# The MLP's way down by seven products of sums of quarters

## The reference, cut to what matters

```python
x = x + squared_relu_mlp(rms_norm(x, mlp_norm[l]), w_up[l], w_down[l])     # l = 0, 1

def rms_norm(x, g):
    return x * lax.rsqrt(jnp.mean(x * x, axis=-1, keepdims=True) + EPS) * g

def squared_relu_mlp(h, w_up, w_down):                   # w_up 1024 x 4096, w_down 4096 x 1024
    return jnp.square(jax.nn.relu(h @ w_up)) @ w_down
```

## Time and profile before

| what | us |
| --- | --- |
| median of three runs | 3433.12 |
| lowest, highest run | 3431.18, 3434.05 |
| profiled execution, span from the first to the last instruction | 3430.4 |
| PE busy | 3379.4 (99%) |
| DVE, POOL, ACT busy | 1962.6, 1260.6, 1205.7 |

### The profile page before, as it was taken

One profiled execution on the slowest core, in us unless ns is written; L12 is line 12 of the kernel. 1 busy time (PEld: TensorE's weight loads), 2 busy tenths in 40 slices (PEclk: granted clock), 3 DMA queues, 4 the chain that ended last, 5 costly groups with the idle time before them and its releaser, 6 DMA issues.

```text
span 3430.4 us, 43111 instructions
## 1 busy us (share of the span) xinstructions
PE 3379.4 (99%) x16026; PEld 2788.4 (81%) x16026; DVE 1962.6 (57%) x2418; ACT 1205.7 (35%) x2072; POOL 1260.6 (37%) x828
## 2 busy tenths in 40 slices
PE   8999999999999999999999999999999999999999
PEld 7778888888888887777888888887888888778887
DVE  6666662844454477884384444457746546545445
ACT  6446651422222245764142222224524233102011
POOL 1121214444445440024344445453435345323340
PEclk9999999999999999999999999999999999999999
DMA  5010012111111121111211111113111111111241
GB/s 214 21 42 18 24 58 86 49 50 50 50 49 50 54 108 60 46 46 65 78 49 50 50 49 50 60 58 107 37 59 58 43 61 45 64 46 62 93 148 66
DMA packets 67634, 211.84 MB, mean 62 GB/s; under 512 B 7280, under 2 KB 11888, under 8 KB 65680
## 3 DMA queue, kind: packets, MB, share of 16 engines
q1 hardware_dynamic: 56848, 165.04, 14.6%
q10 hardware_dynamic: 10624, 44.63, 3.6%
HBM read 186.32 MB, written 22.02 MB: 61 GB/s over the span
## 4 chain that ended last, share of the span: by engine, by line
PE 92%; DVE 5%; issue 1%; POOL 1%; ACT 1%; DMA 1%; ACTq 0%; DVEq 0%; SPq 0%; POOLq 0%
PE G L885 37%; PE G L1303 20%; PE AUX L1253 17%; PE G L1545 3%; PE G L1124 2%; PE AUX L1186 2%; PE AUX L1424 2%; PE AUX L1322 2%; PE AUX L1176 1%; PE G L1007 1%; PE AUX L1166 1%; PE AUX L1053 1%; PE AUX L1303 1%; PE AUX L1506 1%; DVE probs L2553 1%
## 5 line engine op out<-in xcount | busy, mean ns | idle before, releaser
L885 PE MATMUL G<-Hhi,whi 128*128 128x512 f32 x1552 | 631.6, 407 | 7.3 <-DVE Hlo L2682 2.8
L885 PE MATMUL G<-Hhi,wlo 128*128 128x512 f32 x1552 | 605.9, 390 | 0.0
L885 PE MATMUL G<-Hlo,whi 128*128 128x512 f32 x1552 | 605.4, 390 | 0.0
L685 POOL CAST whi<-wraw 128x1024 fp32r<-128x1024 f32 (+1 forms) x123 | 135.6, 1102 | 1101.4 <-PE G L885 592.7
L1303 PE MATMUL G<-u_hi,slot_hi 128*128 128x512 f32 x992 | 387.7, 391 | 0.0
L1303 PE MATMUL G<-u_lo,slot_hi 128*128 128x512 f32 x992 | 386.2, 389 | 0.0
L1303 PE MATMUL G<-u_hi,slot_lo 128*128 128x512 f32 x992 | 386.1, 389 | 0.0
L885 PEld LDWEIGHTS G<-Hhi,whi 128*128 128x128 f32 x1552 | 292.1, 188 | 74.4 <-issue 7.1
L734 POOL TENSOR_TENSOR slot_lo<-raw_down,slot_hi 128x512 fp32r<-128x512 f32 x144 | 190.2, 1321 | 416.4 <-ACT slot_hi L1923 416.2
L885 PEld LDWEIGHTS G<-Hlo,whi 128*128 128x128 f32 x1552 | 292.3, 188 | 62.5 <-issue 5.7
L885 PEld LDWEIGHTS G<-Hhi,wlo 128*128 128x128 f32 x1552 | 291.7, 188 | 61.8
(11 more groups left out here) (463 smaller groups left out, 6890.8 us busy)
## 6 DMA issues: line engine op xcount, KB each, us to landing
wraw<-wjobs SPq DMA_DIRECT2D x148, 512.0 KB, 3.4
raw_down<-down_pairs SPq DMA_DIRECT2D x64, 512.0 KB, 3.4
raw_up<-up_units SPq DMA_DIRECT2D x30, 512.0 KB, 3.7
raw_up<-up_units SPq DMA_DIRECT2D x44, 256.0 KB, 3.3
mw_raw<-wjobs SPq DMA_DIRECT2D x16, 512.0 KB, 5.2
scratch<-X ACTq DMA_DIRECT2D x2, 4096.0 KB, 13.0
gate_tiles<-gate_st ACTq DMA_DIRECT2D x16, 512.0 KB, 4.1
T<-gate_tiles ACTq DMA_DIRECT2D x16, 512.0 KB, 3.5
```

The lines of the kernel that those rows point to most:

```text
L685: pool.tensor_copy(whi[:, par, 0:kt], wraw[:, par, 0:kt]).then_inc(w_hi, 1)
L885: mm = pe.matmul(G[:, par if psum is None else psum, cols], w[:, par, k, :], x[:, k, cols], start=(i == 0 and j == 0), stop=(i == kt - 1 a ...
```

## The change

In chunks 1 to 6 of both layers the way down is made as the way up: the 512 x 1024 piece of u (two units of 256 hidden features) and the matching piece of w_down are cut into quarters, and each of two groups g of output features (256 of each half) takes seven products (`unit_down`) instead of eight. A product is 2 x 2 x 3 = 12 matmuls into 1024 columns of G. `unit_up` replaces `unit` in chunks 1 to 7. In the middle chunks it ends in seven matrices per unit h, each 128 x 512: the blocks b11, b22, b21 of u and the sums t1 = b11 - b12, t2 = b22 + t1, t3 = b22 - b12, t4 = b21 - t2 (`total`, tiles d_sum), their high parts by ScalarE (`high_of_u`, tiles d_hi) and their low parts by VectorE (`low_of_u`, tiles d_lo in the place of d_sum). Each block is squared in place in SBUF (`square`). `add_product` adds each of the fourteen bank contents to a quarter of X; p1, p6, p7 and p4 accumulate in one bank pair, p5 and p3 in the other, and a product that goes on in a bank waits until VectorE has added what stood there.

The weights of the way down come as two more units, through the same raw buffers and `unit_weights` on GpSimd: per unit s1, s3, low of p1, s2, low, low of p6 (p6 comes third in each order), s4 and the remaining lows. `high` and `ahead` on ScalarE go over 28 uses a chunk.

The room for d_hi and d_lo is taken from t4 and from T: b21 and t4 of the input now share one 16 KB place. Both are written once to HBM (operand_tiles) during chunk 0, and `load_shared` fetches the one that is needed next: 2 MB, as four DMAs, in each unit of chunks 1 to 7, after its second product; it is used by that unit's last product (p2 or p4) and by the second product of the next unit.

The factor r2 is no longer applied to each chunk's sum: in chunk 0 X is multiplied by mean square + eps before the first sum is added, chunks 0 to 7 are added unscaled, and after chunk 7 X is multiplied by the reciprocal. The reciprocal stands after chunk 0's additions. Chunks 0 and 7 keep the plain way down; in chunk 7 `finish` makes the four low parts at each unit's end, and ScalarE's copies into T in the second unit wait for all four of the first.

The diff, cut to its core (`after(j, n)` waits for product j and n copies; `factor` is the former `product` with `load_shared`'s semaphore):

```diff
+FACTORS = {"p1": ("a11", "b11"), "p2": ("a12", "b21"), "p3": ("s4", "b22"), "p4": ("a22", "t4"),
+           "p5": ("s1", "t1"), "p6": ("s2", "t2"), "p7": ("s3", "t3")}
+UP_ORDER = (("p1", "p4", "p6", "p5", "p7", "p3", "p2"), ("p1", "p2", "p6", "p5", "p7", "p3", "p4"))
+DOWN_ORDER = ("p1", "p5", "p6", "p3", "p7", "p2", "p4")
+CHAINED = ("p1", "p6", "p7", "p4")
...
+LOW_ORDER = (("t3", "b11", "t1", "b22", "b21", "t2", "t4"), ("b11", "t1", "t2", "b22", "t3", "b21", "t4"))
...
+            def load_shared(n):
+                for half in range(2):
+                    ks = slice(2 * half, 2 * half + 2)
+                    for part in range(2):
+                        sp.dma_start(b21[part][:, ks, :].bitcast(F32), operand_tiles[n, part][:, ks, :]).then_inc(shared_in[half], 16)
...
+                for c in range(1, CHUNKS):
+                    for h in range(2):
+                        sp.wait_ge(m_used, use_of(l, c, h, 1) + 1)
+                        load_shared(1 - h)
+                        if c not in WHOLE:
+                            sp.wait_ge(m_lo, use_of(l, c, h, PRODUCTS - 1) + 1)
+                            load_unit(l, c, 2 + h)
...
+                    else:
+                        pe.wait_ge(m_exit, read)
+                        factor(c, h, 1, 2, True)
+                        pe.wait_ge(m_x, copied + 1)
+                        factor(c, h, 2, a, False)
+                        factor(c, h, 3, 1, True)
+                        pe.wait_ge(m_x, copied + 2)
+                        factor(c, h, 4, a, False)
+                        pe.wait_ge(m_x, copied + 3)
+                        factor(c, h, 5, 1, False)
+                        pe.wait_ge(m_exit, read + 2)
+                        factor(c, h, 6, a, False)
...
+                def unit_down(c, g):
+                    for j, name in enumerate(DOWN_ORDER):
+                        n, op = use_of(l, c, 2 + g, j), FACTORS[name][1]
+                        par, start = g if name in CHAINED else 1 - g, name in ("p1", "p5", "p2")
+                        if name in ("p6", "p7", "p4"):
+                            pe.wait_ge(m_out, added(l, c, g, {"p6": "p1", "p7": "p6", "p4": "p7"}[name]))
+                        elif name in ("p3", "p2"):
+                            pe.wait_ge(m_out, added(l, c, g, {"p3": "p5", "p2": "p3"}[name]))
...
+                        for h in range(2):
+                            if g == 0:
+                                pe.wait_ge(m_ul, f_low(l, c, h, op))
+                            for i in range(2):
+                                w = slice((2 * i + h) * P, (2 * i + h + 1) * P)
+                                for s, (a, x) in enumerate(((slot_hi, d_hi), (slot_hi, d_lo), (slot_lo, d_hi))):
+                                    mm = pe.matmul(G[:, par, i * HALF:(i + 1) * HALF], a[slot_of(n)][:, w], x[h][op][:],
+                                                   start=(start and h == 0 and s == 0), stop=(h == 1 and s == 2),
+                                                   skip_group_check=not start)
+                        mm.then_inc(m_used, 1)
...
+                    copies = ({"p1": ("b11", 0), "p4": ("b21", 2), "p6": ("b12", 0), "p5": ("b22", 1)} if h == 0 else
+                              {"p1": ("b11", 3), "p6": ("b12", 3), "p5": ("b22", 1)})
+                    for j, name in enumerate(UP_ORDER[h]):
+                        n = use_of(l, c, h, j)
+                        if name in copies:
+                            block, bank = copies[name]
+                            act.wait_ge(m_used, n + 1)
+                            if whole and h:
+                                act.wait_ge(m_ul, tiles_to(l, c, 1))
+                            act.copy(block_of_u(c, h, block), AUX[:, bank, :]).then_inc(m_x, 1)
+                        ahead(n)
+                        if h == 0:
+                            if j == 5:
+                                high_of_u(c, 0, "b22", "b21")
+                            elif j == 6:
+                                high_of_u(c, 0, *(("b12", "b11") if whole else ("t3",)))
+                        elif j == 0 and not whole:
+                            high_of_u(c, 0, "b11", "t1", "t2", "t4")
+                        elif j == 2:
+                            high_of_u(c, 1, "b11")
+                        elif j == 5:
+                            high_of_u(c, 1, "b22")
+                        elif j == 6:
+                            high_of_u(c, 1, *(("b12", "b21") if whole else ("t1", "t2", "t3")))
...
+                        for j in range(2 * PRODUCTS):
+                            ahead(use_of(l, c, 2, j))
+                            if j == 0:
+                                high_of_u(c, 1, "b21", "t4")
...
-                chain.link(dve.tensor_tensor(bank, bank, r2[:], ALU.mult))
-                dve.tensor_tensor(X[:, m, :], bank, X[:, m, :], ALU.add).then_inc(m_out, 1)
+                if c == 0:
+                    chain.link(dve.tensor_tensor(X[:, m, :], X[:, m, :], r2[:], ALU.mult))
+                    dve.wait_ge(m_used, use_of(l, c, 2, m) + 1)
+                    dve.tensor_tensor(X[:, m, :], bank, X[:, m, :], ALU.add).then_inc(m_out, 1)
+                else:
+                    dve.wait_ge(m_used, use_of(l, c, 2, m) + 1)
+                    chain.link(dve.tensor_tensor(X[:, m, :], bank, X[:, m, :], ALU.add))
+                    dve.tensor_tensor(X[:, m, :], X[:, m, :], r2[:], ALU.mult).then_inc(m_out, 1)
...
+                    if h == 0:
+                        after(4, 4)
+                        dve.tensor_tensor(b22_, a, b22_, ALU.subtract).then_inc(m_exit, 1)
+                        dve.tensor_tensor(b21_, a, b21_, ALU.add).then_inc(m_exit, 1)
+                        square("b22", 1)
+                        square("b21", 2)
+                        after(5, 4)
+                        dve.tensor_tensor(b12_, b12_, d, ALU.subtract).then_inc(m_exit, 1)
+                        square("b12", 3)
+                        total("t3", "b22", "b12", ALU.subtract, "b12")
+                        after(6, 4)
+                        dve.tensor_tensor(b11_, e, b11_, ALU.add).then_inc(m_exit, 1)
+                        square("b11", 4)
+                        total("t1", "b11", "b12", ALU.subtract, "b11")
+                        total("t2", "b22", "t1", ALU.add, "t1")
+                        total("t4", "b21", "t2", ALU.subtract, "t2")
+                        if whole:
+                            finish()
+                        else:
+                            dve.wait_ge(h_sums, f_sum(l, c, h, "t4"))
+                            low_of_u(*LOW_ORDER[0])
...
+                    after(1, 1)
+                    dve.tensor_tensor(b11_, e, b11_, ALU.add).then_inc(m_exit, 1)
+                    square("b11", 1)
+                    after(4, 3)
+                    dve.tensor_tensor(b22_, a, b22_, ALU.subtract).then_inc(m_exit, 1)
+                    square("b22", 2)
+                    after(5, 3)
+                    dve.tensor_tensor(b12_, b12_, d, ALU.subtract).then_inc(m_exit, 1)
+                    square("b12", 3)
+                    total("t1", "b11", "b12", ALU.subtract, "b12")
+                    total("t2", "b22", "t1", ALU.add, "t1")
+                    if not whole:
+                        low_of_u("b11")
+                    total("t3", "b22", "b12", ALU.subtract, "b12")
+                    if not whole:
+                        dve.wait_ge(h_sums, f_sum(l, c, h, "t3"))
+                        low_of_u("t1")
+                    after(6, 3)
+                    chain.link(dve.tensor_scalar(b21_, a, 0.0, None, ALU.max))
+                    dve.scalar_tensor_tensor(b21_, a, 0.0, b21_, ALU.max, ALU.mult).then_inc(h_sums, 1)
+                    total("t4", "b21", "t2", ALU.subtract, "b21")
+                    if whole:
+                        finish()
+                        return
+                    dve.wait_ge(h_sums, f_sum(l, c, h, "t4"))
+                    low_of_u("t2")
+                    add_product(c, 0, 0)
+                    low_of_u("b22")
+                    add_product(c, 0, 1)
+                    low_of_u("t3", "b21")
+                    add_product(c, 0, 2)
+                    low_of_u("t4")
...
+                    if name in ("p5", "p3"):
+                        ins = dve.tensor_tensor(x, x, bank, ALU.subtract)
+                    else:
+                        ins = dve.tensor_tensor(x, bank, x, ALU.add)
+                    ins.then_inc(m_out, 1)
```

More of the change, by code:

```diff
@@ L84 @@
 PRODUCTS = 7
-CHUNK_USES = 2 * PRODUCTS + KT
-MLP_USES = CHUNKS * CHUNK_USES
+WHOLE = (0, CHUNKS - 1)
+MIDDLE = CHUNKS - len(WHOLE)
+CHUNK_USES = [2 * PRODUCTS + (KT if c in WHOLE else 2 * PRODUCTS) for c in range(CHUNKS)]
+USES_BEFORE = [sum(CHUNK_USES[:c]) for c in range(CHUNKS)]
+MLP_USES = sum(CHUNK_USES)
 BLOCKS = ("11", "22", "12", "21")
@@ L397, in build, with block_of_u @@
```

(54 more changed lines are left out.)

362 lines of the change are left out of this document (269 added, 93 removed).

## The result

The changed kernel takes 3524.26 us (median of 4 runs, 3523.11 to 3525.39), the kernel before 3432.69 in the runs beside them (4 runs): a ratio of 1.0268, 95% interval 1.0253 to 1.0283. It is slower by 92 us; 3509 was predicted, with 3405 to 3545 as the range.

The account below looks back on a forecast made before the run. TensorE, busy 99%, was taken as the bound; fewer matmuls but new waits on VectorE and ScalarE: 3430.4 + 66 (middle chunks) + 7.8 (chunk 7) + 2 (last tile) = 3506, plus 2.7 to the runs' median: 3509 us, range 3405 to 3545.

Parts of the forecast that it names:

- The lock: VectorE operations with two SBUF inputs take turns with GpSimd's instructions: one of each costs 1.29 + 0.42 = 1.71 us.
- The walk: Step-by-step timing of one middle chunk from its first up unit: 10.98 us of TensorE waits, chunk 87.3 us, 5.5 more.
- Its 3.37 us: Unit 2's product 6 waits for ScalarE's copy of p5's bank, behind the cast of b11: 36.65 instead of 33.28.
- the 0.64 of b11's bank: Second unit's product 2 overwrites the bank of b11, so it starts at 22.40 instead of 21.76: 0.64 us wait.
- The 1.07 for p1's weight: On a middle chunk's way down, product p1 waits 1.07 us for its weight's low, ending at 43.06.
- The 0.68 for the low of t1: On a middle chunk's way down, p5's second half waits 0.68 us for the low of t1, at 50.42.
- Chunk 7: Copy into T waits for all four lows, 2.6 us; last lows end 1.3 late: 3.9 a layer, 7.8 in all.
- The tail: Product with r2 moves from PSUM to two SBUF operands, hidden until the last tile: 1 us a layer, 2 in all.
- items at nothing: Chunk 0's multiply of X, the 6.55 us reciprocal in chunk 1, and the operand stream and its writing: all expected hidden.
- The first: Rival: GpSimd's instructions slip past while VectorE waits for products, TensorE stays the bound: 77.2 us a chunk, 3380; chance 0.22.
- The second: Rival: ScalarE's cast of b11 is in time, waits of 4.5 to 8 us a chunk: 3431 to 3473; chance 0.12.
- The third: Rival: the streamed half lands late, last product of the first unit waits 2.3 us, fourteen times: 3541; chance 0.06.

Follow-up runs that it names:

- the last experiment: Changed kernel with t1 to t4 and squared b12 in PSUM, unit 1's lows later, unit 2 in TensorE's order, chunk 7's unit 2 blocks placed apart: 3375.33 us, 0.9833.
- the fifth run: Changed kernel with the differences t1 to t4 and the squared b12 kept in idle PSUM banks, all work still done: 3422.57 us, 0.9969 of the kernel before.
- the sixth run: Changed kernel with t1 to t4 and squared b12 in PSUM, and ScalarE's cast of unit 2's b11 one product later: 3412.33 us, 0.9943.
- the third run: Changed kernel with the streamed up operands' transfers fetching 8 of 512 columns, output not the reference's: 3523.78 us, 1.0268 of the kernel before.
- the first run: Changed kernel with GpSimd's weight sums and lows in chunks 1 to 7 on 8 of 512 columns, output not the reference's: 3379.53 us, 0.9853.

## Why the prediction was right

Its direction and mechanism held; it came out 15 us too fast.

*Removed work.* 24 matmuls a chunk at 0.2274 us: shown by the last experiment, whose chunk is within 0.4 of the 76.29 that the prediction gives to a TensorE that never waits.

*The lock.* Right, and the 1.71 us of a pair too: VectorE's sums and lows that meet GpSimd follow each other at 1.70 to 1.75 from start to start in the chain above (987.71 and 989.41, 1010.71 and 1012.46). With one input in PSUM they don't take turns: in the fifth run these operations take 0.67 to 0.70 us beside a GpSimd at full work, those with two in SBUF 1.1 to 1.6.

*The walk.* Counted from 964.26, product 6 of unit 2 starts at 36.59 (walk: 36.65), after the wait that ScalarE's copy behind the cast of b11 was to cause. Its 3.37 us are 2.9 in the rows of waits (3.0 from start to start), and the 0.64 of b11's bank is 0.6. Up to there the walk is exact to 0.1 us. Behind it everything is late by the same amount: the low of b11 ends at 48.20 (47.02), the add of p1 to X at 55.63 (54.42), 1.2 us each.

*The step that was missing.* TensorE's clock. The walk priced all matmuls at 0.2274 us. Product 6 took 4.63 in the chain, 1.6 us more than at the full clock; VectorE's sum of b12 waits for it, and with that sum the rest of the chunk moved. The square behind it gave 0.4 back (1.19 instead of 1.57), which leaves the 1.2. So a chunk became 88.6 instead of 87.3.

The trace holds the test of this. In one of the twelve middle chunks the clock did not fall in product 6:

```profile
2120.64 13.62 PE AUX L1460 x60
2157.23 3.03 PE AUX L1460 x12
2173.75 1.21 DVE X L3188
2175.01 32.94 PE G L1521 x144
```

Product 6 starts at 36.59 again, the add of p1 to X ends at 54.32 (walk: 54.42), and the chunk takes 87.31 (walk: 87.27): here the walk is exact to 0.1 us at its end as well. The other eleven chunks, with 4.27 to 5.50 us for product 6, take 87.84 to 88.65. The second fall is there in this chunk too (a granted clock of 0.83 from 2165 to 2175) and costs nothing: it lies ahead of the wait for the add to X, which takes it up.

Two waits of the walk are missing in the chunk from 964.26. The 1.07 for p1's weight didn't appear because TensorE came later to it; in the chunk from 2120.64 a wait of 0.8 stands at this place. The 0.68 for the low of t1 didn't appear because that low met no instruction of GpSimd (0.69 us, where the chunk from 2120.64 has 1.66); the sum t4 behind it met one in its place (1.80, there 0.74), so the add to X was no earlier for it.

*Chunk 7.* Forecast +3.9, measured 1317.66 - 1230.12 - 81.75 = 5.8. The two waits are there, 2.6 and 1.1. Most of the rest is the clock again, in the chain's own rows: 60 matmuls behind the wait of 2.6 us take 15.54 us, 60 ahead of it 13.62. In the sixth run, whose clock stayed up behind the same wait, they take 13.95.

```profile
1230.12 13.62 PE AUX L1460 x60
...
1256.54 0.59 ACT T L2272
...
1257.18 15.54 PE AUX L1460 x60
```

*The tail and the items at nothing.* The twelve middle chunks have a mean of 88.35 us (six from 699.61 to 1230.12, six from 1854.76 to 2384.39), 6.6 over before; with chunk 7 twice that is 12 x 6.6 + 11.5 = 90.7 of the 92.4 us by which the span grew. 1.7 are left for all else. The tail's 2 fit into that, though no run shows the tail alone. The reciprocal lies in chunk 1, which takes 88.17 and 88.65 us and so no longer than the other middle chunks: it is hidden. For the stream the third run shows it; in the changed kernel the loads landed after 6.4 and 6.8 us in median, inside the 5 to 9.

*The size.* Against the walk's 3506 the span is 16.8 us longer: 12 x (88.35 - 87.27) = 13 from the middle chunks and 11.5 - 7.8 = 3.7 from chunk 7, in the main the clock in both.

*The rivals.* The first (the lock is rarely met) is refuted by the 1.5 us of the sums. Its 3380 is, though, what the first run gave with the lock taken away, 3379.5: its price was right and its condition wrong. The second asked for b11's square by 32; it ended at 35.4. The third is refuted by the third run.

## What to carry to other kernels

Before VectorE is given work in SBUF beside a busy GpSimd, count its operations with two SBUF inputs and price each that meets GpSimd at GpSimd's instruction plus the gap, here 1.29 + 0.42 = 1.71 us instead of 0.69; keeping one input in an idle PSUM bank brought the operation back to 0.67 to 0.70 us, and it won more here (102 us) than any single order (10 to 33). An order pays as well: 27 and 32 us while VectorE was short of time, with most of the wait coming back at another product, and 10 to 33 after that. The last and largest of these follows what TensorE asks for next. A wait of TensorE is not worth its length alone: look at the granted clock behind it, price the next product at the lower clock as well (here 0.43 instead of 0.227 us a matmul), and ask whether the end waits for that product. Here the first fall cost 1.3 us a chunk and the second nothing.

## What the runs showed that I had not expected

- Waits of TensorE of 2.6 to 3.8 us are mostly followed by matmuls at 0.43 instead of 0.227 us, with the granted clock, in the changed kernel, at 0.74 and 0.83 of full speed over stretches of 6 and 7 us. But not always: behind the 2.8 us in the chunk from 2120.64 the clock stayed up for two products (1.00 from 2157 to 2165), and behind the 2.6 us of chunk 7 it fell in the fifth run and not in the sixth (0.91 and 1.00 from 1195 to 1215). In the runs with the differences in PSUM, whose waits are 1.2 us at most in the middle chunks, those chunks show 1.00. What exactly decides was not tried.
- A stall moves. Of the 2.9 us at ScalarE's copy, 2.1 came back at another product when the copy was freed, and 3.8 when VectorE's lows were put behind the square of b11, in both cases at a sum on which the prediction had put no wait.
- Destination and inputs differ: with both inputs in SBUF the square into PSUM took 1.57 us, the difference with one input in PSUM 0.69.
